# Eleven filler tiles moved to earlier passes of the attention loop of a two-layer trunk

## The reference

```
gates, aq, ak, av, bq, bk, bv, cin = split(h @ w_in)
out_a = gqa(...)                      # branch 0: 8 heads, softmax attention
out_b = rms_norm(diff_attention(...)) # branch 1: softmax(s1) - lam * softmax(s2), 4 heads
out_c = rwkv7_bidir(cin, ...)         # branch 2
up = einsum('btim,imd->btid', [out_a, out_b, out_c], w_up)
out = sum(sigmoid(gates) * up, over the 3 branches) @ w_out
```

## Time and profile before

| | |
|---|---|
| median of 3 runs | 2877.86 us (2876.57 to 2886.07) |
| the profiled execution | 2877.86 us, its span 2875.7 us |
| PE, PEld busy | 2611.5 us (91%), 2407.1 us (84%) |
| DVE, ACT, POOL busy | 1494.0 us (52%), 1037.4 us (36%), 318.1 us (11%) |
| mean granted TensorE clock | 0.942 |

### The profile page before, as it was taken

How to read it: one execution, slowest core, us unless ns; L and a number is a source line. 1 busy time by engine, 2 the same in 40 slices (tenths; PEclk the granted TensorE clock), 3 DMA queues, 4 the chain that set the end, 5 groups by cost and what they waited for, 6 DMA issues and landing times. The chain is left out here.

```text
span 2875.7 us, 56425 instructions
## 1 busy us (share of the span) xinstructions
PE 2611.5 (91%) x23140; PEld 2407.1 (84%) x23140; DVE 1494.0 (52%) x2487; ACT 1037.4 (36%) x1675; POOL 318.1 (11%) x312
## 2 busy tenths in 40 slices
PE   5999999899778888999989999989987888899998
PEld 4888989887677778999968899988876778789996
DVE  3434455555567756443453344665466666554434
ACT  3333244343523323432243323534344233243322
POOL 0000131000022212100100001300000222040001
PEclk7999999998899998999989999999988899999999
DMA  7765533332200013446366654432221000234463
GB/s 254 228 217 189 167 103 111 87 90 59 70 13 3 3 28 88 119 131 187 108 213 212 206 183 125 126 96 81 83 59 59 3 3 3 64 96 127 128 205 99
DMA packets 481770, 318.35 MB, mean 111 GB/s; under 512 B 15442, under 2 KB 438888, under 8 KB 481384
## 3 DMA queue, kind: packets, MB, share of 16 engines
q1 hardware_dynamic: 481512, 314.73, 36.0%
HBM read 311.28 MB, written 3.41 MB: 109 GB/s over the span
## 5 line engine op out<-in xcount | busy, mean ns | idle before, releaser
L787 PE MATMUL acc<-xm_hi,w_hi 128*128 128x384 f32 x2512 | 871.1, 347 | 41.9 <-POOL xm_lo L1745 14.3
L789 PE MATMUL acc<-xm_hi,w_lo 128*128 128x384 f32 x2512 | 853.3, 340 | 0.0
L788 PE MATMUL acc<-xm_lo,w_hi 128*128 128x384 f32 x2448 | 831.0, 339 | 0.0
L1860 DVE TENSOR_TENSOR w_lo<-raw,w_hi 128x1024 fp32r<-128x1024 f32 (+1 forms) x420 | 515.9, 1228 | 488.3 <-ACT w_hi L1395 480.8
L1395 ACT ACTIVATE w_hi<-raw 128x1024 fp32r<-128x1024 f32 (+1 forms) x420 | 438.8, 1045 | 312.5 <-PE acc L789 216.7
L787 PEld LDWEIGHTS acc<-xm_hi,w_hi 128*128 128x128 f32 x2512 | 483.3, 192 | 69.6 <-issue 43.6
L789 PEld LDWEIGHTS acc<-xm_hi,w_lo 128*128 128x128 f32 x2512 | 482.6, 192 | 0.0
L788 PEld LDWEIGHTS acc<-xm_lo,w_hi 128*128 128x128 f32 x2448 | 470.4, 192 | 1.5
L787 PE MATMUL acc<-h_hi,w_hi 128*128 128x384 f32 x704 | 241.0, 342 | 9.3 <-DVE w_lo L1860 9.3
L788 PE MATMUL acc<-h_lo,w_hi 128*128 128x384 f32 x704 | 238.7, 339 | 0.0
L789 PE MATMUL acc<-h_hi,w_lo 128*128 128x384 f32 x704 | 238.5, 339 | 0.0
(11 more groups left out here) (341 smaller groups left out, 3456.4 us busy)
## 6 DMA issues: line engine op xcount, KB each, us to landing
raw<-in_ffn_w_in SPq DMA_DIRECT2D x179, 512.0 KB, 3.9
modw<-in_w_mod SPq DMA_DIRECT2D x71, 1024.0 KB, 6.1
raw<-in_w_in SPq DMA_DIRECT2D x114, 512.0 KB, 4.1
raw<-in_ffn_w_out SPq DMA_DIRECT2D x64, 512.0 KB, 4.7
raw<-in_ffn_w_out SPq DMA_DIRECT2D x32, 384.0 KB, 3.6
raw<-in_w_up SPq DMA_DIRECT2D x24, 512.0 KB, 3.5
modx<-in_w_mod SPq DMA_DIRECT2D x9, 1024.0 KB, 13.0
raw<-in_w_out SPq DMA_DIRECT2D x16, 512.0 KB, 4.2
```

What stands on the lines that cost most here:

```text
L787: pe.matmul(out, lhs[0], rhs[0], start=first, stop=False)
L788: pe.matmul(out, lhs[0], rhs[1], start=False, stop=False)
L789: return pe.matmul(out, lhs[1], rhs[0], start=False, stop=last)
L1860: done(dve.tensor_tensor(w_lo[:, c % SPL, 0:w], raw[:, c % RAW, 0:w], w_hi[:, c % SPL, 0:w].bitcast(F32), ALU.subtract), lo_done)
```

## The change

Only `plan_fillers` is changed. `b0` is 24, the first pass of branch 1, and `KD` is 8.

```diff
     for m in range(KD):
         fill[NB + m] += [("rot", 5 + m), ("g", 0, m)]
         fill[NB + KD + m].append(("g", 1, m))
-        fill[b0 if m == 0 else b0 + 4 + m].append(("g", 2, m))
+        fill[b0 if m == 0 else b0 + 2 + m].append(("g", 2, m))
     for mp in range(KD // 2):
-        fill[b0 + 1 + mp].append(("u", 0, mp))
+        fill[b0 + 1 + mp // 2].append(("u", 0, mp))
     return fill
```

## The result

The changed kernel takes 2900.93 us (median of 7 runs, 2893.16 to 2904.03) against 2880.31 (2876.57 to 2886.07) for the kernel before in the same rounds: ratio 1.0066, 95% interval 1.0051 to 1.0083. That is about 19 us slower, where +5.7 was forecast with a range up to +13. Its profiled execution took 2898.49 us, span 2896.7. The work is the same: 56425 instructions, VectorE and ScalarE busy for 1493.2 and 1037.4 us. The mean granted clock of TensorE is 0.936, before 0.942.

The account below looks back on a forecast made before the run. TensorE, busy for 91% of the span, was taken as the bound, except where VectorE's chain sets the end. 8.56 - 1.83 - 2.76 - 1.49 + 0.35 = +2.83 us a layer, +5.7 on 2877.86: 2883.5 us, range 2877 to 2891.

Parts of the forecast that it names:

- 2 x 4.28: Passes 25 and 26: each takes a second filler of 4.28 us, so pass 27 starts 8.56 us later.
- The pair 28-29: Passes 28 and 29, holding g2 and g3 instead of u3 and g1: 17.66 us falls to 15.83, gain 1.83.
- The end of tile 7: Stretch behind pass 35: stays at 12.40 us except that its transposes go at half rate, +0.35 us.
- clock term: Pass 30 at TensorE's full clock instead of 0.64: gain 2.76 us a layer.
- Pass 30: Takes 5.84 us instead of 8.60, with a 2.63 us stall before it and the full clock: gain 2.76.
- The clock falls in front of pass 30 all the same: Rival: pass 30 stays at 8.60 us; 2886.3 us if one layer (chance 0.13), 2889.0 if both (0.21).
- Passes 34-35: Without fillers the reciprocal starts 2.40 us earlier, a table load loses 0.91: net gain 1.49 us a layer.
- the 2.66 of the Trainium skill: Rival for pass 35's table switch: about 2.3 us lost instead of 0.91, 2886.3 us in all, chance 0.02.
- Passes 31-32: Passes 31 and 32 hold the same kinds of work as before: no change in time.
- Late weights: Rival in passes 25 and 26: second fillers wait 2.28 us each for their chunk's split; 2892.6 us, chance 0.05.
- Empty passes that cost nothing: Rival: stalls in front of passes 30 and 33 go too, 2 x 2.63 us a layer less; 2873.0 us, chance 0.06.

Follow-up runs that it names:

- two kernels with every stall filled: Kernel before and changed kernel, each with extra matmuls of constants in TensorE's stalls from pass 20 to tile 7's end: ratios to before 0.9930 and 0.9971.
- each half of the change: Kernel before with only the u fillers paired in passes 25 and 26: ratio 1.0024; with only gate fillers g1 to g7 moved to passes 27 to 33: 1.0017.
- the first experiment: Kernel before and changed kernel measured and profiled once more with no edit: ratios 1.0004 and 1.0063.
- the tail version: Kernel before with gate fillers g6 and g7 put behind the sums of tile 7, passes 30 and 33 empty: ratio 0.9994.

## Why the prediction was wrong

**The cause that it gave is right.** "2 x 4.28" for passes 25 and 26 measured 8.30 to 8.34 us a layer in every profile; the second filler of a pass adds 4.16 us and not 4.28, since the 4.28 took in a first matmul of 0.44 us, where most others took 0.34. TensorE's idle time there is 0.18 us as forecast, no weights were late, and pass 27 started 20.42 us behind pass 25, with 20.7 forecast. The pair 28-29 gave back 1.81 and 1.82 (1.83). The end of tile 7 cost 0.35 (0.35). The prediction's sum without its clock term is 8.56 - 1.83 - 1.49 + 0.35 = 5.59 a layer. The two kernels with every stall filled test it: from pass 25 to the first matmul of `up(1, 0)` they take 96.55 and 92.25 us in layer 1, 4.3 apart, and with the 1.56 that the latter's pass 30 lost to the clock 5.9 apart; layer 2 gives the same. The times say no more than that it is of this size: 0.9971 - 0.9930 = 0.0041 is 5.9 us a layer, but the two intervals together leave it anywhere from about 3 to 9. That this figure meets the sum is partly luck, since it holds parts outside of the attention too.

**The step that failed is "Pass 30": "I take the 2.63 us stall and the full clock: gain 2.76".** The stall came out at 2.63 us to the hundredth. The clock didn't follow from it. It had held behind this stall in front of pass 33, twice in the one profile, and I took two layers as two observations (and it held there twice more when the kernel before was profiled again). In the changed kernel it was at half behind the same stall in front of pass 30 in three of four cases. In its place the runs show that a stall of this length doesn't decide by itself: pass 30 takes 8.6 or 5.84 us, pass 33 takes 5.84 or 7.4, and in all seven cases in which pass 30 went at the full clock and the stall in front of pass 33 was left at 2.63, pass 33 did not. These are one in the changed kernel's second profile, two in each half of the change, and two in the kernel before with five extra matmuls. What differs between such cases is what ran before and the time at which the work falls; which of the two decides isn't shown.

The length of a stall counts too: behind all ten stalls in front of passes 30 and 33 that extra matmuls cut to 1.33 us, with fillers in these passes, the clock held, and behind 1.99 it held twice and fell within pass 30 twice. Filling the stalls with matmuls made passes 30 and 33 of the changed kernel 5.84 in both layers and that kernel some 10 us faster.

The Trainium skill (TensorE: Matmul & The Clock Gate, section Part 1: The HAM clock gate) says that the monitor of TensorE's activity runs freely, not started with the kernel, so that the place of a change varies from run to run. The 8.69 and 5.84 us in the two layers of one execution fit this, but no run sets the monitor against the work, so it is an explanation and not a finding here.

**How much of the miss this step is.** On the mean of the four layers profiled, the clock in pass 30 cost 2.1 us a layer against the forecast, that is 4.2 of the 13 us between +5.7 and +19. Pass 33 adds 1.6, passes 31-32 and 34-35 together 1.3, and passes 25-26 take 0.5 off. The rest lies outside of the stretch or in executions that weren't profiled, as said below.

**The rival that came nearest had the mechanism, but too low a price.** "The clock falls in front of pass 30 all the same" was priced at 2.76 in each layer and 2889.0 us at most, chance 0.34 in one or both. It left out that the same stall in front of pass 33 could fall too (+1.56 and +1.58, in one layer of each profile of the changed kernel) and that the kernel's other runs have a higher base than the profiled execution: the medians of before were 2880 to 2884 in the rounds of the result and the later ones, against the 2877.86 that I added to. The range, up to 2891, should have had both.

**Smaller terms.** Passes 34-35 gave 1.17 and not 1.49. TensorE was busy for 6.69 us there in layer 1, where 4.3 to 5.5 had been forecast, because the clock was at half for most of it (0.66 on the mean); the path didn't go through it. The reciprocal started 5.50 us in (forecast 5.45), and the table load did stand behind the maxima, as ScalarE in the order of time, in the changed kernel, shows:

```profile
769.83 1.28 ACT L1540 ACT_TABLE_LOAD   x1 [1.27 <-DVE st L2096]
```

VectorE in the same stretch, the reciprocal and the maxima:

```profile
764.22 2.55 DVE L2128 RECIPROCAL t<-t 128x384 f32<-128x384 f32 x1 [0.88 <-ACT t L1553]
...
768.73 0.56 DVE L2095 TENSOR_REDUCE st<-pb 128x1 f32<-128x384 f32 x1
```

From 768.73 to the transposes at 773.67 are 4.94 us, against 3.74 in the last pass before: the load costs 1.20 there, as in the rows, and not the 2.66 of the Trainium skill (ScalarE: Activation LUTs, section What ACT_TABLE_LOAD costs). I had taken 4.65 from another pass, 0.29 too few. Passes 31-32 cost 0.35 more, which was put at nothing. VectorE idles 2.33 us in front of its subtraction in pass 31 and 1.98 in pass 28, at the same place in the work. The profile names ScalarE's copy of the high part, but that isn't late: it ends 0.46 us before the subtraction in pass 31 (740.57 + 1.06) and 0.10 before it in pass 28 (716.15 + 1.06). What VectorE waits for is open. These are the two subtractions, on VectorE in the changed kernel:

```profile
717.31 1.23 DVE L1860 TENSOR_TENSOR w_lo<-raw,w_hi 128x1024 fp32r<-128x1024 f32 x1 [1.98 <-ACT w_hi L1395]
...
742.09 1.23 DVE L1860 TENSOR_TENSOR w_lo<-raw,w_hi 128x1024 fp32r<-128x1024 f32 x1 [2.33 <-ACT w_hi L1395]
```

**The other rivals.** Late weights: excluded by the rows of passes 25 and 26. Empty passes that cost nothing: the stalls stayed at 2.63.

**What stays open.** From pass 25 to the end of `up(1, 0)` the changed kernel is 13.5 us longer in the first pair of profiles and 10.9 in the second, both layers together, 12.2 on the mean. Outside it is 3.6 us longer on the mean, with the clock as told in the first experiment. The time differs by 18 to 19. So some 3 us aren't placed. They may lie in executions with a lower clock than the two that were profiled: these took 2898.49 and 2892.33 us, both less than the medians of 2900.93 and 2898.36. Why the clock outside falls more in some executions is open, and so is whether the changed order makes it fall more often there. In the tail version, too, 9 us of gain in the stretch shrank to 2 in the time, which the interval doesn't separate from none.

## What to carry to other kernels

Filler work is worth its length where another engine's chain sets the end, and costs its length where the main engine does: list the passes by which engine is busy all along, and move work by that list, one pass at a time. Don't credit a moved stall with a change of TensorE's clock because the clock held behind an equal stall elsewhere in one profile; take both levels as ends of the term. A gain or loss read from one stretch needn't arrive in the whole time: compare the rest of the execution too. If TensorE's stalls are short and scattered, a few matmuls on constants in them can be worth more than any move of real work: here 0.7%, as much as the whole change lost.

## What the runs showed of the hardware

Behind a stall of 2.63 us, in front of a pass of the same kind (one filler, 5.84 us at the full clock), the clock was at half at once (8.58 to 8.69 us for pass 30), or fell in the middle of the pass (7.35 to 7.45 for pass 33), or held (5.83 to 5.86). Half the clock on one pass of short products costs 1.1 us even when TensorE isn't busy all along: passes 21 to 23 took 3.78 us with extra matmuls and 4.86 without, though each has 0.9 us of stall. And a part with no edit differs between executions of one kernel: behind layer 2's `up(1, 0)` the kernel before took 677.6 us at a granted clock of 0.94 and 684.4 at 0.93, so that what one profile leaves over can be off by 5 us or more.
